# Two layers of a streaming encoder on one core: other places for a gate, a split and three transposes between the mixing heads and w_out

## The reference

```python
h = rms_norm(x, gains[0]) * (1 + sc1) + sh1
x = x + MACARON_W * ga1 * rms_norm(swiglu(h, w_f1_in, w_f1_out), gains[1])
h = rms_norm(x, gains[2]) * (1 + sc2) + sh2
y, rows = token_mixing(h, ..., w_in, w_gate, b_gate, g_gla, w_out)
x = x + ga2 * rms_norm(y, gains[3])
h = rms_norm(x, gains[4]) * (1 + sc3) + sh3
x = x + MACARON_W * ga3 * rms_norm(swiglu(h, w_f2_in, w_f2_out), gains[5])
```

## Time and profile before

| what | value |
|---|---|
| median of 3 runs | 1660.62 us (1658.96 to 1661.53) |
| the profiled execution | 1660.62 us, of which the span of its instructions is 1659.0 us |
| PE busy | 1593.5 us (96%) |
| DVE busy | 813.0 us (49%) |
| ACT busy | 580.0 us (35%) |
| POOL busy | 151.5 us (9%) |
| chain that ended last | PE 86%, DVE 6%, ACT 3%, DMA 2% |

### The profile page before, as it was taken

One profiled execution on the slowest core, in us unless ns is written; L12 is line 12 of the kernel. 1 busy time (PEld: TensorE's weight loads), 2 busy tenths in 40 slices (PEclk: granted clock), 3 DMA queues, 4 the chain that ended last, 5 costly groups with the idle time before them and its releaser, 6 DMA issues.

```text
span 1659.0 us, 25807 instructions
## 1 busy us (share of the span) xinstructions
PE 1593.5 (96%) x10150; PEld 1450.5 (87%) x10150; DVE 813.0 (49%) x1147; ACT 580.0 (35%) x781; POOL 151.5 (9%) x227
## 2 busy tenths in 40 slices
PE   4999999989998899999999999999999988999998
PEld 2999998879987799998879999987999868999986
DVE  3433442358667634443364444335675775444424
ACT  3322222363454522222262222224535534222222
POOL 5000000010332000000010000000105210000000
PEclk7999999999999999999999999999999999999999
DMA  9577744653345477444557744355533263444432
GB/s 349 179 239 233 232 127 152 222 146 103 102 132 180 125 228 228 127 126 147 185 177 228 229 127 126 127 180 176 153 114 112 72 229 85 124 127 124 136 125 77
DMA packets 252694, 266.01 MB, mean 160 GB/s; under 512 B 11679, under 2 KB 216605, under 8 KB 252610
## 3 DMA queue, kind: packets, MB, share of 16 engines
q1 hardware_dynamic: 230512, 183.52, 36.8%
q0 software_dynamic: 22080, 81.26, 14.2%
q10 hardware_dynamic: 18, 0.04, 0.0%
HBM read 258.70 MB, written 6.09 MB: 160 GB/s over the span
## 4 chain that ended last, share of the span: by engine, by line
PE 86%; DVE 6%; ACT 3%; DMA 2%; DVEq 1%; SPq 1%; issue 1%; ACTq 0%
PE ps L1792 19%; PE ps L1794 19%; PE ps L1793 19%; PE ps L1837 7%; PE ps L1839 7%; PE ps L1841 7%; PE ps L1755 2%; DVE x L1272 1%; DMA w_raw<-in_w_ffn_in_dram 1%; DMA w_ada_g<-in_w_ada_dram 1%; ACT square_out L829 1%; SPq L508 1%; DMA w_raw<-in_w_in_dram 0%; PE ps L1854 0%; DVE gate_tok L1178 0%
## 5 line engine op out<-in xcount | busy, mean ns | idle before, releaser
L1792 PE MATMUL ps<-act_hi,w_hi 128*128 128x384 f32 x1696 | 572.7, 338 | 0.0
L1794 PE MATMUL ps<-act_hi,w_lo 128*128 128x384 f32 x1696 | 567.3, 334 | 0.0
L1793 PE MATMUL ps<-act_lo,w_hi 128*128 128x384 f32 x1696 | 566.9, 334 | 0.0
L1233 DVE TENSOR_TENSOR w_lo<-w_raw,w_hi 128x2048 fp32r<-128x2048 f32 x158 | 363.7, 2302 | 234.9 <-ACT w_hi L874 206.5
L1792 PEld LDWEIGHTS ps<-act_hi,w_hi 128*128 128x128 f32 x1696 | 318.4, 188 | 10.3 <-issue 9.9
L874 ACT ACTIVATE w_hi<-w_raw 128x2048 fp32r<-128x2048 f32 x128 | 245.3, 1917 | 227.5 <-PE ps L1841 226.8
L1793 PEld LDWEIGHTS ps<-act_lo,w_hi 128*128 128x128 f32 x1696 | 318.6, 188 | 0.0
L1794 PEld LDWEIGHTS ps<-act_hi,w_lo 128*128 128x128 f32 x1696 | 318.4, 188 | 0.0
L927 ACT ACTIVATE silu_g<-ps 128x384 f32<-128x384 f32 x88 | 43.3, 492 | 552.2 <-PE ps L1794 552.2
L1309 DVE TENSOR_TENSOR hid_f<-silu_g,ps 128x384 f32<-128x384 f32 x88 | 48.8, 554 | 381.8 <-ACT silu_g L927 381.8
L1837 PE MATMUL ps<-w_hi,hid_hi 128*128 128x512 f32 x528 | 164.2, 392 | 0.0
(11 more groups left out here) (386 smaller groups left out, 1437.3 us busy)
## 6 DMA issues: line engine op xcount, KB each, us to landing
w_raw<-in_w_ffn_in_dram SPq DMA_DIRECT2D x176, 512.0 KB, 5.1
w_ada_sb<-in_w_ada_dram POOLq DMA_DIRECT2D x45, 1024.0 KB, 7.1
w_raw<-in_w_ffn_out_dram SPq DMA_DIRECT2D x88, 512.0 KB, 4.1
w_raw<-in_w_in_dram SPq DMA_DIRECT2D x46, 512.0 KB, 4.7
w_ada_g<-in_w_ada_dram POOLq DMA_DIRECT2D x16, 1024.0 KB, 5.5
w_raw<-in_w_out_dram SPq DMA_DIRECT2D x16, 512.0 KB, 5.9
w_ada_g<-in_w_ada_dram SPq DMA_DIRECT2D x5, 1024.0 KB, 11.8
w_ada_s<-in_w_ada_dram POOLq DMA_DIRECT2D x3, 1024.0 KB, 9.7
```

Source lines behind the costliest of these rows:

```text
L1233: dve.tensor_tensor(w_lo[slot][:], w_raw[slot][:], w_hi[slot][:].bitcast(F32), ALU.subtract).then_inc(lo_ready.sem, 1)
L1792: pe.matmul(out, w, a, start=first, stop=False)
L1793: pe.matmul(out, w, al, start=False, stop=False)
L1794: return pe.matmul(out, wl, a, start=False, stop=last)
```

## The change

The change moves work inside the hand-written lists. Nothing is added or removed except one wait.

- ACT: the silu of the GLA gate comes ahead of the four sigmoids. The copies of the prompt values (`mix_prompts`) come behind the copies of the turned sample weights. The rounded part of the third `w_out` unit is made behind all four GLA copies.
- DVE: the low part of the DSA output and three memsets come ahead of the masking of the GLA scores. The low part of the third `w_out` unit is made behind all GLA work, ahead of `spread_gate`.
- PE: the transposes of the sample weights of group A come ahead of the prompt values. `gates_to_tokens(1, 1)` comes ahead of the third and fourth `w_out` unit.
- POOL: the wait for all ten `weights_ready` goes, so the GLA gate is applied as soon as each head is copied.

```diff
--- before.py
+++ after.py
@@ -788,7 +788,6 @@
                 for h in range(HB):
                     if h == 0:
                         pool.wait_ge(silu_r_ready.sem, silu_r_ready.at(l, 1))
-                        pool.wait_ge(weights_ready.sem, weights_ready.at(l, 10))
 
                     pool.wait_ge(gla_copied.sem, gla_copied.at(l, h + 1))
                     pool.tensor_tensor(gla_out[:, h, :], gla_out[:, h, :], U[:, RB + h, :], ALU.mult).then_inc(gla_gated.sem, 1)
@@ -1089,11 +1088,11 @@
 
                 act.drain()
                 act.activation(act_hi[:, 6:8, :], dsa_out[:], ACT.Copy).then_inc(dsa_hi.sem, 1)
+                act.wait_ge(u_odd.sem, u_odd.at(l, NU // 2))
+                act.activation(U[:, RB:RB + 4, :], U[:, RB:RB + 4, :], ACT.Silu).then_inc(silu_r_ready.sem, 1)
                 for h in range(HA):
                     act.wait_ge(z_mm.sem, z_mm.at(l, 5 + h + 1))
                     act.activation(keep[:, h, :], ps[:, 4 + h, 0:N], ACT.Sigmoid, scale=-QSCALE).then_inc(keep_ready.sem, 1)
-                act.wait_ge(u_odd.sem, u_odd.at(l, NU // 2))
-                act.activation(U[:, RB:RB + 4, :], U[:, RB:RB + 4, :], ACT.Silu).then_inc(silu_r_ready.sem, 1)
                 act.wait_ge(z_mm.sem, z_mm.at(l, 10))
                 act.activation(keep_s[:, 0:3, :], ps[:, 0, 0:3 * NK].rearrange("p (i k) -> p i k", k=NK), ACT.Sigmoid, scale=-QSCALE)
                 act.activation(keep_s[:, 3, :], ps[:, 1, 0:NK], ACT.Sigmoid, scale=-QSCALE).then_inc(keep_ready.sem, 1)
@@ -1119,11 +1118,11 @@
                 copy_turned(3)
                 square_and_scale(2)
                 square_and_scale(3)
-                mix_prompts(0)
-                mix_prompts(1)
                 act.wait_ge(wt_tr.sem, wt_tr.at(l, 5))
                 act.activation(sb_swT[:], ps[:, 2, :].rearrange("p (i r) -> p i r", r=P), ACT.Copy)
                 new_weights(3, wt_ready)
+                mix_prompts(0)
+                mix_prompts(1)
                 for h in range(HB):
                     act.wait_ge(gla_mean_mm.sem, gla_mean_mm.at(l, h + 1))
                     act.activation(gla_stds[h], ps[:, 4 + h, 0:N], ACT.Sqrt, bias=eps_col).then_inc(gla_std.sem, 1)
@@ -1132,10 +1131,9 @@
                 for h in range(HB):
                     act.wait_ge(gla_f32.sem, gla_f32.at(l, h + 1))
                     act.activation(act_hi[:, 2 + h, :], gla_out[:, h, :], ACT.Copy).then_inc(gla_hi.sem, 1)
-                    if h == 1:
-                        split_hi(U_WOUT + 2, (U_WOUT + 2) % 2)
-
-                split_hi(U_WOUT + 3, (U_WOUT + 3) % 2)
+
+                for u in range(U_WOUT + 2, U_F2IN):
+                    split_hi(u, u % 2)
 
                 act.wait_ge(gla_lo.sem, gla_lo.at(l, HB))
                 split_first_hi(U_F2IN, U_WOUT + 1)
@@ -1582,6 +1580,11 @@
                 w_in_unit(10, spread_sb_queries)
                 w_in_unit(11)
 
+                dve.wait_ge(dsa_hi.sem, dsa_hi.at(l, 1))
+                dve.tensor_tensor(act_lo[:, 6:8, :], dsa_out[:], act_hi[:, 6:8, :].bitcast(F32), ALU.subtract).then_inc(dsa_lo.sem, 1)
+                dve.memset(rest[:, :, P:P + 1], 1.0)
+                dve.memset(rest[:, :, N + 1:N + 2], 1.0)
+                dve.memset(rest_s[:, :, NK:NK + 1], 1.0)
 
                 att_v = att[:].rearrange("p t (c e n) -> p t c e n", c=2, e=2)
                 for kind in range(2):
@@ -1606,9 +1609,6 @@
                     ins.then_inc(states_ready.sem, 1)
                     dve.drain()
 
-                dve.memset(rest[:, :, P:P + 1], 1.0)
-                dve.memset(rest[:, :, N + 1:N + 2], 1.0)
-                dve.memset(rest_s[:, :, NK:NK + 1], 1.0)
                 for h in range(HA):
                     dve.wait_ge(keep_ready.sem, keep_ready.at(l, h + 1))
 
@@ -1640,8 +1640,6 @@
                     dve.tensor_tensor(act_lo[:, 2 + h, :], gla_out[:, h, :], act_hi[:, 2 + h, :].bitcast(F32),
                                       ALU.subtract).then_inc(gla_lo.sem, 1)
 
-                dve.wait_ge(dsa_hi.sem, dsa_hi.at(l, 1))
-                dve.tensor_tensor(act_lo[:, 6:8, :], dsa_out[:], act_hi[:, 6:8, :].bitcast(F32), ALU.subtract).then_inc(dsa_lo.sem, 1)
                 mix_low_prompts(0)
                 mix_low_prompts(1)
                 invert_gla_std(0)
@@ -1662,8 +1660,6 @@
                 for h in range(HB):
                     if h >= 2:
                         invert_gla_std(h)
-                    if h == 2:
-                        split_lo(U_WOUT + 2, (U_WOUT + 2) % 2)
 
                     dve.wait_ge(gla_gated.sem, gla_gated.at(l, h + 1))
                     dve.tensor_tensor(gla_out[:, h, :], gla_out[:, h, :], gla_stds[h], ALU.mult).then_inc(gla_f32.sem, 1)
@@ -1673,6 +1669,7 @@
 
                 dve.wait_ge(rows_stored.sem, rows_stored.at(l, 10))
                 dve.wait_ge(states_stored.sem, states_stored.at(l, 4))
+                split_lo(U_WOUT + 2, (U_WOUT + 2) % 2)
                 spread_gate(1)
                 read_gate(1, 0)
                 read_gate(1, 1)
@@ -1854,7 +1851,7 @@
                         m = pe.transpose(ps[:, 6 + f // 4, (f % 4) * P:(f % 4 + 1) * P], rows, ident[:])
                     m.then_inc(gate_tr.sem, 1)
 
-                def last_two(u, chunks, src_hi, src_lo, nth, ready, turn_gates=None):
+                def last_two(u, chunks, src_hi, src_lo, nth, ready):
 
                     def products(n, k):
                         for kc in range(2):
@@ -1865,8 +1862,6 @@
                     split_ready(u)
                     products(0, 0)
                     products(0, 1)
-                    if turn_gates is not None:
-                        turn_gates()
                     ready(1)
                     split_ready(u + 1)
                     products(1, 0).then_inc(y_done.sem, 1)
@@ -2213,13 +2208,14 @@
                 pe.wait_ge(keep_ready.sem, keep_ready.at(l, 5))
                 turn_weights(2)
                 turn_weights(3)
+                pe.wait_ge(weights_ready.sem, weights_ready.at(l, 10))
+                pe.wait_ge(wt_ready.sem, wt_ready.at(l, 2))
+                for i in range(PAIRS):
+                    pe.transpose(ps[:, 2, i * P:(i + 1) * P], keep_s[:, i, 0:PAST], ident[:])
+                turn_new_weights(keep_s, 3, wt_tr)
                 pe.wait_ge(wt_ready.sem, wt_ready.at(l, 4))
                 for c in range(2):
                     prompt_values(sb_wT, SB_PV_BANK, c, lambda t, h: TM[:, t, TM_VA + 64 * h:TM_VA + 64 * h + 64])
-                pe.wait_ge(weights_ready.sem, weights_ready.at(l, 10))
-                for i in range(PAIRS):
-                    pe.transpose(ps[:, 2, i * P:(i + 1) * P], keep_s[:, i, 0:PAST], ident[:])
-                turn_new_weights(keep_s, 3, wt_tr)
                 for h in range(HB):
                     pe.wait_ge(gla_copied.sem, gla_copied.at(l, h // 2 * 2 + 2))
                     pe.matmul(ps[:, 4 + h, 0:N], ones_v[:], gla_sqs[h], start=True, stop=True).then_inc(gla_mean_mm.sem, 1)
@@ -2245,11 +2241,12 @@
                     for tile in TILES:
                         m = tile_products((U_WOUT + 1) % 2, tile, act_hi, act_lo, WOUT_CHUNKS[1] + kc, kc, False, False)
                 m.then_inc(unit_used.sem, 1)
+                gates_to_tokens(1, 1)
 
                 def gla_ready(n):
                     pe.wait_ge(gla_lo.sem, gla_lo.at(l, WOUT_CHUNKS[2 + n]))
 
-                last_two(U_WOUT + 2, WOUT_CHUNKS[2:4], act_hi, act_lo, 1, gla_ready, lambda: gates_to_tokens(1, 1))
+                last_two(U_WOUT + 2, WOUT_CHUNKS[2:4], act_hi, act_lo, 1, gla_ready)
                 if l < LAST:
                     for g in range(len(LOOP_F2)):
                         four_hidden(U_F2IN, KF, 2, 4 * g, lambda qs: ada_quarters(N_F2 + g, qs), N_F2 + g,
```

## The result

The changed kernel takes 1673.99 us (median of 4 executions, 1673.36 to 1676.48), the kernel before 1661.07 us in 4 executions beside it (1658.96 to 1664.63): 1.008 times as long, with a 95% interval of 1.0067 to 1.0091. The profiled execution took 1675.07 us, its span 1673.5 us, 14.5 us more than before.

A forecast was written before the change was run, and what follows sets the result against it. PE, busy nearly throughout, was taken as the bound, with one stretch of waits per layer between `w_in` and the second feed-forward network. 2 x 7.05 + 0.4 = 14.5 us on 1660.6 gave 1675 us, range 1663 to 1681.

The forecast's parts named there:

- W: The moment in each layer when PE starts `w_out`; the tail is counted from it.
- order of silu, subtraction, transposes: Ahead of `w_out`: `keep_s` ready and resumed on 1.2 us later, `mix_prompts` on ACT 0.75 more; 1.95 us per layer.
- POOL's gates in DVE's chain: Without its wait, POOL's four gates fall between DVE's last `keep` and `keep_s` instructions and delay them: 3.6 us per layer.
- cold clock behind the wait: PE idles 5.6 us ahead of `keep_s`, so its clock falls to 1.2 GHz: 1.5 us per layer, ends 0 and 2.5.
- W late, sum: The start of `w_out` comes 1.95 + 3.6 + 1.5 = 7.05 us later in each layer.
- W to the first gating: From the start of `w_out` to DVE gating the first finished tile: -0.3 us in layer 0, +0.7 in layer 1.
- the rival that scans take no harm: POOL disturbs only DVE's plain subtractions and maxima; `w_out` about 4 us late per layer, 1669 us; chance 0.20.
- the row of seven instructions: DVE's two-input instructions from 1309.8 on: end of last head, mask, four scans, subtraction; room for all four POOL gates.
- My bound of 2.5 from the tail of layer 0: Two tile products after a 3.79 us wait in `w_out` took 5.2 us instead of 2.75: 2.5 us lost.
- my rival at 1665: POOL costs DVE nothing on the chain, and PE's 2.0 us wait leaves the clock up: 1665 us; chance 0.13.
- the load rival: The later load for the second feed-forward network takes 14 us and becomes the bound: 1685 us; chance 0.08.
- the faster rival: The tail's wait for the gates is short or leaves the clock up, nothing in `w_out` runs cold: 1657 us; chance 0.07.

The follow-up runs named there:

- both at once: Changed kernel with POOL's wait for the tenth `weights_ready` put back and 16 identity transposes on PE in the wait for `keep_s`: 1663.63 us, 1.0012.
- the last split: Kernel before, with DVE making the low part of the last `w_out` unit ahead of the second `read_gate` instead of behind it: 1667.3 us, 1.0035.

## Why the prediction was right

The changed kernel was to take 1675 us and took 1674, for the reasons given, but two of the terms were wrong in size and cancel: POOL's was 0.8 to 1.6 us per layer too large and the clock's 0.9 to 1.2 too small. That the sum is right to a microsecond is luck. Per layer, in us; the measured first term is that of "both at once", the second the difference in the start of the `keep_s` transposes to it, the third the difference in the way from there to W:

| term | predicted | layer 0 | layer 1 |
|---|---|---|---|
| order of silu, subtraction, transposes | 1.95 | 2.1 | 2.0 |
| POOL's gates in DVE's chain | 3.6 | 2.8 | 2.0 |
| cold clock behind the wait | 1.5 | 2.4 | 2.7 |
| W late, sum | 7.05 | 7.3 | 6.6 |
| W to the first gating | -0.3 / +0.7 | -0.56 | +0.34 |

Both layers and their tails give 13.8 us. The last projection copy of layer 0, ahead of all the edits in that layer, was itself 1.1 us late in this execution, which makes 14.9, and elsewhere 0.4 us come back: 14.5. The 14.5 of the forecast is met by the profiled execution (1675.07); by the medians the change costs 12.9.

**The silu, the subtraction, the order on PE.** Confirmed: sigmoids 2.0 late, PE idle for 2.9 us (3.0 predicted), and 2.0 to 2.1 us at W, made of 1.3 / 1.1 for DVE (1.2 predicted) and 0.9 for the values behind the transposes (0.75 predicted).

**POOL in DVE's chain.** The mechanism is shown by the two kernels that differ in the one wait; the rival that scans take no harm has fallen: the row of its eight scans gives 458 to 1214 ns each, where the same row of before (the first of these two) has 465 to 491:

```profile
L1629 DVE TENSOR_TENSOR_SCAN rest_s<-keep_s,ones_row x8: 465/466/491, 496.3 to 1310.3; 128x160 f32<-128x160 f32 x8
...
L1629 DVE TENSOR_TENSOR_SCAN rest_s<-keep_s,ones_row x8: 458/794/1214, 499.5 to 1320.4; 128x160 f32<-128x160 f32 x8
```

The mis-sized step is that the row of seven instructions is "enough for each gate to get in": the term is 2.8 / 2.0, not 3.6. The scans lost 1.39 us and the subtraction 0.56, in layer 0 the mask another 0.82. Not every gate found something to hold up: between the second and the third POOL waits 0.82 / 0.62 us for ACT's next copy, and the last ends after `keep_s` is done (1320.40 + 2.82 against 1320.97 + 1.39). How many scans are met differs between executions: with 30 filling transposes, where DVE and POOL run as in the changed kernel, the `keep_s` transposes start 2.8 us later in both layers than in "both at once".

**The clock.** It fell as predicted, but I sized it at 1.5 and it was 2.4 / 2.7. I had let a part of it hide under ACT's copies; in the changed kernel PE has hardly any idle time from the `keep_s` transposes to W, so its own way, values and means, is the chain there, and all of the cold clock counts. My bound of 2.5 from the tail of layer 0 would have been the better value. The view behind my rival at 1665, that about 2 us of waiting leave the clock at 2.4 GHz, does not hold: in four kernels it falls after waits of 1.79 to 2.16 us, though one of these kernels keeps it after 2.25 us in its other layer.

**The tail.** As predicted: the wait moved ahead of the gates (3.61 / 3.24 instead of 4.0), the split of the last unit is hidden, and the load landed at the latest 7.6 us after its issue (7 predicted). It is hidden by little: in layer 1 `first_lo` ends at W + 32.3, not at the W + 30.7 of the forecast, 0.1 us ahead of the gating. The edits in `w_out` alone changed nothing, so the load rival and the faster rival have both fallen, the faster one because the wait ahead of the gates brings the clock down as the old wait did.

What I had not thought of is that the parts do not add up. The median against the kernel beside it is +12.9 us for the whole, but +7.1 for POOL's wait alone, +10.1 for the silu alone (from executions that lie 7 us apart) and +5.6 for the subtraction alone. The first two each open a hole in PE that costs the clock by itself, and the subtraction costs clock at W without a new hole. In the whole change the hole ahead of the products L2187 is split in two and costs no clock, and the second fall is absorbed: behind W PE waits for DVE's gates anyway.

Left open: why the clock falls ahead of W while PE is busy. It does so in both layers of the changed kernel, with POOL's wait back, with the sigmoids first again and with the subtraction alone, and in one layer of four others; among these is the kernel that is edited only behind W ("the last split", 0.60 from 1321 to 1324), so the edits need not be its cause. It does not in the other six, the kernel before and the one with 30 filling transposes among them. Open too is what decides whether a wait brings the clock down. Waits of 0.96, 1.57, and 1.19 + 1.71 us leave it up and 1.80 takes it down, but with the values put back 2.25 us leave it up in layer 0 and 2.16 take it down in layer 1, so the length alone does not decide. Whether the work ahead of the wait does was not tried.

## What to carry to other kernels

A wait of about two microseconds on a busy TensorE can cost twice, and in these runs mostly did: read the granted clock behind it, and if nothing useful fits, see what a few transposes into an unused bank give. A wait that looks needless on GpSimd may be what keeps it away from the two-input instructions of DVE that PE waits for; look at what would coincide before taking it out. And removing a wait only pays if the instruction ahead of the next hand-over is moved as well: the same edit made this kernel about 5 us slower alone and 9 to 10 us faster with a second one.

## What the runs showed of the hardware

- DVE's scan of 128 x 160 with two operands took 0.47 us alone and up to 1.21 us in the changed kernel (1.30 with the values put back) beside a GpSimd operation of 128 x 384; GpSimd's took 0.99 alone and up to 1.57.
- After one wait of 2.95 us, in the longest of seven executions, TensorE ran at 1.2 GHz for more than ten microseconds under gapless small products (0.50 over 1306 to 1316), which took 2.5 to 3.5 us a group instead of 1.6 to 1.9. After single waits of 1.80 to 2.16 us (three kernels) it was at 1.2 GHz for between three and four microseconds; after one of 2.25 us it stayed up.
- A table load took 1.28 us on ACT, and the next activation started 1.29 to 1.30 us after the load did; silu and sigmoid each needed one.
